# Accumulation ahead of the mixer steps, alternating PSUM banks, and a long convolution over 13 weight items: one change to a two-block kernel on one core

## The reference, cut to what matters

```
# block 1: h = x + token_mixer(rms_norm(x)); h = h + conv_gated_mlp(rms_norm(h)); rms_norm
proj = n @ w_in                       # per head: q,k,v,z of a gated delta rule (4 tiles of 128),
                                      # and q,k,v of 3 dilated attentions (9 tiles)
mixed = concat(delta_mixer(...), dilated_mixer(...)) @ w_out
# block 2, modulated: shift, scale and gate from two condition vectors
m = silu(c) @ w_ada + b_ada           # 2048 x 12288, for two vectors c
u = modulate(rmsnorm(x), sh1, sc1);  p = u @ w_in_2
a = hgrn2_mixer(p[:5 parts], context) # per head 5 tiles
y = x0 * long_conv(x1 * v)            # "hyena", per head 3 tiles, by Fourier transforms
x = x + g1 * (concat(a, y) @ w_out_2);  x = x + g2 * mlp(modulate(rmsnorm(x)))
```

## Time and profile before

| | before |
|---|---|
| time, median of 3 runs | 3736.71 us (3734.02 to 3743.41) |
| profiled execution | 3737.85 us, of it span 3736.1 us |
| PE busy | 3350.2 us (90%) |
| DVE busy | 2304.9 us (62%) |
| ACT busy | 1557.9 us (42%) |
| POOL busy | 1427.2 us (38%) |
| DMA | 672.83 MB, mean 180 GB/s |

### The profile page before, as it was taken

How to read it: one execution, slowest core, us unless ns; L and a number is a source line. 1 busy time by engine, 2 the same in 40 slices (tenths; PEclk the granted TensorE clock), 3 DMA queues, 4 the chain that set the end, 5 groups by cost and what they waited for, 6 DMA issues and landing times.

```text
span 3736.1 us, 58829 instructions
## 1 busy us (share of the span) xinstructions
PE 3350.2 (90%) x21604; PEld 3013.0 (81%) x21604; DVE 2304.9 (62%) x3370; ACT 1557.9 (42%) x2196; POOL 1427.2 (38%) x672
## 2 busy tenths in 40 slices
PE   5898989898979999999987887888887999999998
PEld 4888988898877878878864886788887788888886
DVE  5676666766655883883874755666665654535353
ACT  4344333433334443443433554344433443434343
POOL 2334433343323444444431333344433344444442
PEclk7999999999999999999998998898988999999999
DMA  4655565556455555556544755565554655565553
GB/s 167 198 171 177 175 205 168 177 173 205 165 194 194 184 174 188 178 171 191 179 137 150 233 182 186 173 199 157 167 166 187 227 181 183 180 191 186 186 186 112
DMA packets 262366, 672.83 MB, mean 180 GB/s; under 512 B 28263, under 2 KB 66888, under 8 KB 261448
## 3 DMA queue, kind: packets, MB, share of 16 engines
q1 hardware_dynamic: 262152, 669.81, 54.7%
HBM read 663.38 MB, written 6.32 MB: 179 GB/s over the span
## 4 chain that ended last, share of the span: by engine, by line
PE 55%; DVE 18%; issue 14%; POOL 5%; ACT 4%; DMA 3%; SPq 1%; DVEq 1%; ACTq 0%; POOLq 0%
PE psum L633 20%; PE psum L634 10%; POOL w_lo L495 5%; PE psum L626 4%; PE psum L628 4%; PE psum L627 4%; ACT w_hi L485 2%; PE psum L703 2%; DVE w_lo L495 2%; DVE psum L476 1%; PE psum L631 1%; PE psum L1396 1%; PE psum L1405 1%; DVE work L1252 1%; DVE work L1631 1%
## 5 line engine op out<-in xcount | busy, mean ns | idle before, releaser
L495 POOL TENSOR_TENSOR w_lo<-raw,w_hi 128x1024 fp32r<-128x1024 f32 (+3 forms) x668 | 1427.0, 2139 | 2278.9 <-ACT w_hi L485 2278.1
L485 ACT ACTIVATE w_hi<-raw 128x1024 fp32r<-128x1024 f32 (+3 forms) x1112 | 1046.4, 947 | 1394.2 <-PE psum L628 663.8
L626 PE MATMUL psum<-act_a,w_lo 128*128 128x256 f32 x3072 | 929.1, 302 | 62.5 <-ACT work L663 36.8
L495 DVE TENSOR_TENSOR w_lo<-raw,w_hi 128x1024 fp32r<-128x1024 f32 (+3 forms) x444 | 541.4, 1219 | 576.9 <-ACT w_hi L485 575.0
L627 PE MATMUL psum<-act_a,w_hi 128*128 128x256 f32 x3072 | 891.7, 290 | 0.0
L628 PE MATMUL psum<-act_a,w_hi 128*128 128x256 f32 x3072 | 891.3, 290 | 0.0
L633 PE MATMUL psum<-act_a,w_hi 128*128 128x512 f32 x2295 | 829.6, 403 | 25.2 <-DVE act_a L745 10.6
L633 PE MATMUL psum<-act_b,w_hi 128*128 128x512 f32 x2096 | 754.6, 402 | 27.7 <-DVE act_b L1639 17.9
L626 PEld LDWEIGHTS psum<-act_a,w_lo 128*128 128x128 f32 x3072 | 612.6, 199 | 74.3 <-ACT work L663 32.9
L634 PE MATMUL psum<-act_a,w_lo 128*128 128x256 f32 x2295 | 648.1, 282 | 0.0
L627 PEld LDWEIGHTS psum<-act_a,w_hi 128*128 128x128 f32 x3072 | 612.8, 199 | 3.1 <-issue 1.9
(11 more groups left out here) (335 smaller groups left out, 3319.8 us busy)
## 6 DMA issues: line engine op xcount, KB each, us to landing
raw<-w_mlp SPq DMA_DIRECT2D x256, 512.0 KB, 3.8
raw<-w_up SPq DMA_DIRECT2D x176, 512.0 KB, 3.5
raw<-w_dil SPq DMA_DIRECT2D x192, 384.0 KB, 3.4
work<-w_ada SPq DMA_DIRECT2D x288, 256.0 KB, 4.0
raw<-w_hg SPq DMA_DIRECT2D x128, 320.0 KB, 3.0
raw<-w_delta SPq DMA_DIRECT2D x64, 512.0 KB, 3.9
raw<-w_out SPq DMA_DIRECT2D x64, 512.0 KB, 5.9
raw<-w_down SPq DMA_DIRECT2D x64, 512.0 KB, 3.6
```

The costliest lines, as they stand in the source:

```text
L485: act.activation(w_hi[:, t % SPLIT, 0:nb * P], raw[:, t % RAW, 0:nb * P], ACT.Copy)\
L495: eng.tensor_tensor(w_lo[:, t % SPLIT, 0:nb * P], raw[:, t % RAW, 0:nb * P], w_hi[:, t % SPLIT, 0:nb * P], ALU.subtract)\
L626: pe.matmul(bank[:, 0:S], wl, src[:, kt, 0:S], start=first, stop=False)
```

## The change

1. `Phase("one", ..., unroll=2)`, and `bank` with two banks adds the head's parity: head 0 puts tiles 0, 1, ... 12 into banks 0, 1, ... 0, head 1 into banks 1, 0, ... 1. `bank_free_after` asks for the last tile of the head before in the same bank. With 8 tiles a head, `two` keeps its banks.
2. On DVE the accumulation steps of an item stand at its start, ahead of the split and the mixers. In `one` the places move from items 2 to 15 (two in 6 and 11) to 3 to 15 (two in 5, 9 and 13), in the pair phases (`ctx`, `out`, `out2`) similarly; in `two` they stay at 0 to 15. `ADA_LAG` is 7 for 8.
3. `ada_finish` takes 3 steps instead of 2: ACT in the first, PE and DVE in the third. In `two` it starts at item 18 instead of 16.
4. The convolution takes 13 items instead of 6: DVE's steps in items 1, 5, 7, 10 and 12 (were 0, 2, 3, 4, 5), PE's in 4, 6 and 9 (were 2, 3, 4), ACT's in 11 (was 4). Its spectra are loaded at SP's item 20 (was 16).

```diff
-ADA_SLOTS, ADA_LAG = 4, 8
+ADA_SLOTS, ADA_LAG = 4, 7
...
-            at = [p for p in range(2, 16) for _ in range(2 if p in (6, 11) else 1)]
+            at = [p for p in range(3, 16) for _ in range(2 if p in (5, 9, 13) else 1)]
...
-            at = range(8) if par else (2, 3, 4, 4, 5, 6, 6, 7)
+            at = range(8) if par else (3, 4, 4, 5, 5, 6, 6, 7)
...
-        last = max(q for q in range(self.tpb) if self.bank(q) == self.bank(k))
+        last = max(q for q in range(self.tpb) if self.bank(q, 1 - self.par) == self.bank(k))
...
-    def bank(self, k):
+    def bank(self, k, par=None):
+        if self.banks == 2:
+            return (k + self.tpb * (self.par if par is None else par)) % 2
...
-        Phase("one", NH, [("w_delta", 8)] * 8 + [("w_dil", 6)] * 24, [KT] * 13, banks=2),
+        Phase("one", NH, [("w_delta", 8)] * 8 + [("w_dil", 6)] * 24, [KT] * 13, banks=2, unroll=2),
...
                 for t in range(ph.ipb):
+                    for idx, (at, _, _) in enumerate(ph.ada_plan(ph.par) if ada else ()):
+                        if at == t:
+                            ada_step(eng, ph, i, idx)
                     if t + AHEAD < ph.ipb:
                         split(eng, ph, i, t + AHEAD)
...
                     for q in range(2):
                         hop(live, q)
-                    for idx, (at, _, _) in enumerate(ph.ada_plan(ph.par) if ada else ()):
-                        if at == t:
-                            ada_step(eng, ph, i, idx)
...
-            return [(0, 6, 1, hyena(eng), -1), (16, 2, 1, ada_finish(who, eng, ph), 0),
+            return [(0, 13, 1, hyena(eng), -1), (18, 3, 1, ada_finish(who, eng, ph), 0),
                     (13, 11, 1, lambda i: hgrn(ph.late)(i), 0)]
...
-            return [(0, 2, 1, ada_finish(who, eng, ph, 1), -1), (0, 8, 1, dilated(eng), -1),
-                    (16, 2, 1, ada_finish(who, eng, ph, 0), 0), (3, 29, 1, delta(eng), 0)]
+            return [(0, 3, 1, ada_finish(who, eng, ph, 1), -1), (0, 8, 1, dilated(eng), -1),
+                    (16, 3, 1, ada_finish(who, eng, ph, 0), 0), (3, 29, 1, delta(eng), 0)]
```

More of the change, by code:

```diff
@@ L573, in body @@
                         if not (first and off < 0):
+                            par, ph.par = ph.par, (ph.par + off) % 2
                             evac(i + off, k)
+                            ph.par = par
                     live = [m for m in live if m[0] > t] + mixers.start(t, i, first)
@@ L588, in drive @@
                 if off < 0:
+                    ph.par = (ph.n - 1) % 2
                     evac(ph.n - 1, k)
+                    ph.par = 0
             mixers.finish(ph.n)
@@ L837, in act @@
                 yield
+                yield
             def pe(i):
+                yield
                 yield
@@ L2176, in gen @@
             def gen(i):
-                for _ in range(4):
+                for _ in range(11):
                     yield
@@ L2187, in gen @@
             def gen(i):
-                yield
-                yield
+                for _ in range(4):
+                    yield
                 pe.wait_ge(sem("two_loaded"), 16 * TWO_LOADS)
@@ L2280, in one_mixers @@
             ph = PHD["one"]
-            return [(0, 2, 1, ada_finish(who, eng, ph, 1), -1), (0, 8, 1, dilated(eng), -1),
-                    (16, 2, 1, ada_finish(who, eng, ph, 0), 0), (3, 29, 1, delta(eng), 0)]
+            return [(0, 3, 1, ada_finish(who, eng, ph, 1), -1), (0, 8, 1, dilated(eng), -1),
+                    (16, 3, 1, ada_finish(who, eng, ph, 0), 0), (3, 29, 1, delta(eng), 0)]
         def pair_mixers(who, eng, ph):
-            return [(0, 2, 1, ada_finish(who, eng, ph), -1)]
+            return [(0, 3, 1, ada_finish(who, eng, ph), -1)]
         block = es.enter_context(nc.Block())
```

2 lines of the change are left out of this document (1 added, 1 removed).

## The result

The changed kernel takes 3694.67 us (median of 4 runs, 3688.78 to 3700.39), the kernel before 3738.21 us on the same chip: ratio 0.9887, 95% interval 0.9869 to 0.9906. That is 42 us less, 1.1%, where 85 were forecast. The profiled execution has a span of 3696.1 us, 40.0 less than before.

The account below looks back on a forecast made before the run. PE, busy 3350.2 of 3736.1 us, was taken to bound the kernel, so gains come from its idle or half-clock time. 3737.85 - 47 - 10 - 28 = 3653, put at 3652 us for the median; range 3610 to 3710.

Parts of the forecast that it names:

- Part A: Phase `one`, head boundaries: alternating banks remove PE's copy-out wait, leaving a 1.9 us scores wait at full clock; 47 us.
- Saved: 6.7 us ... 7 boundaries: 7 x 6.7: Phase `one`: item 1 ends at about 313.1 instead of 319.78 us, at each of 7 boundaries; 47 us.
- moves from item 1 to item 2, ahead of the 5.95 us wait on L1310, which covers it: Phase `one`: L845, the row's turning on PE, 0.95 us at full clock, was to be hidden in that wait.
- Part B: Phase `two`, row of modulation: later finish removes the 5.4 us wait at the row's turning; 1.3 us a head, 10 us.
- So a wait of 5.1 us replaces one of 5.4 ... 1.3 us a head: Phase `two`: PE waits for DVE's products at L2072 instead of the row; 8 heads, 10 us.
- My bounds (-3 to +45): Row of modulation in `two`: -3 us without DVE's earlier chain, +45 with early products and the clock staying up.
- Part C: Phase `two`, convolution over 13 items: transposes' wait falls to 3.6 us, clock likely up; 4.0 us in 7 heads, 28 us.
- What was to cost nothing: Accumulations ahead of splits, weight loads, w_ada loads one item earlier, pair phases, moved copy L2180: 0 us.
- Rival (5): DVE waits for a w_ada transfer ahead of a split PE needs; slower, 3801 us at 8.5 us each; chance 0.05.
- Rival (3): Waits only change names: banks gain 27 us, row loses 3, convolution gains 7; 3707 us; chance 0.20.
- 3610 to 3710: Whole kernel's time: range holding the as-worked-out case, most of the waits-change-names case and nearer part of the waits-vanish case.

Follow-up runs that it names:

- e5_acc_behind: Changed kernel with DVE's accumulations put behind the mixer steps again, all else as changed: ratio 0.9836.
- e1_banks: Kernel before with the alternating banks in `one` alone: 3704.76 us against 3740.85, ratio 0.9901.
- e9_two_early: Changed kernel with the old finish (two steps, from item 16) in phase `two` only: 3664.24 us, ratio 0.9805.
- e3_acc: Changed kernel with banks and convolution of before; accumulations ahead, lag 7, new places, three-step finish and item 18 kept: 3759.60 us, ratio 1.0053.
- e2_conv: Kernel before with the convolution over 13 items and its spectra at item 20 alone: 3698.99 us, ratio 0.9886.
- e10: Changed kernel with the old finish in `two` and the accumulations behind the mixer steps: 3654.17 us against 3739.35 before, ratio 0.9768.
- e6: Kernel before with the alternating banks and the 13-item convolution together, nothing else: 3666.51 us, ratio 0.9791.
- e7: Changed kernel with the two-step finish of before in all phases, from item 16 in `two`: ratio 0.9823.
- e12: Changed kernel with `two`'s splits of items 20 and 21 moved from POOL to DVE, item 23's from DVE to POOL: 3665.11 us, ratio 0.9808.
- e8: Changed kernel, POOL computing `w_lo` of five items a head in `two` for one block only, output partly wrong: one execution, 3653 us.

## Why the prediction was wrong in size and right in sign

**Part A (47 us, came to 33.2; the banks alone 38.9).** The mechanism held: no copy-out waits, scores waiting 2.0 us in five heads, clock at 1.00 behind them. What failed are two steps, "Saved: 6.7 us ... 7 boundaries: 7 x 6.7" and L845, which "moves from item 1 to item 2, ahead of the 5.95 us wait on L1310, which covers it".

The 6.7 us were read off one head. From L1386 (lines of before) to the end of item 1 (ACT's split behind L1532) that head took 81.2 us, but the seven took 80.3 on average. In the changed kernel it is 74.6, near the 74.5 that the forecast implies, so 5.7 us are saved and not 6.7: 7 us in seven heads. In these 74.6 lies a new wait of 0.8 us a head at L1432, since an accumulation now stands ahead of the copy that PE needs; e5_acc_behind, without it, takes 73.4 to 73.9 us in five heads. In the other two it takes 75.7, with the clock at 0.72 behind the scores.

L845 is covered only in part. From the end of item 1 to the next L1386 it is 44.6 us before and in e1_banks, which doesn't move it, and 45.1 in most heads of e5_acc_behind and of the changed kernel, which do. The wait at L1396 stays at 5.9 us. That is 0.5 us in six heads: 3 us.

In two heads, behind the loop's back edge, that second stretch takes 47.6 us. PE waits 2.10 us instead of 1.34 at L1597 and goes on at half clock (its twelve products take 4.54 us for 2.87): 2 x 2.4 = 5. So 47 - 7 - 3 - 5 = 32, and 33.2 were measured. Timelines of DVE and PE at L1432, changed kernel:

```profile
403.00 0.73 DVE L478 SCALAR_TENSOR_TENSOR psum<-work,ada_c,psum 128x512 f32<-128x512 f32 x1
403.65 0.41 DVE L1337 COPY work<-psum 128x256 f32<-128x256 f32 x1
...
404.11 0.71 PE L1432 MATMUL psum<-work 128*128 128x128 f32 x4 [0.80 <-DVE work L1337]
```

e1_banks and e5_acc_behind have no such wait and take 837 us in `one`.

**Part B (10 us, came to a loss: 9 us against before, and some 27 beside part C).** This is the step that failed most: "So a wait of 5.1 us replaces one of 5.4 ... 1.3 us a head". Two things were wrong in it. I put the end of L2002 15.6 us behind the start of L2061 (2382.4 less 2366.8); measured are 17.7 us (2354.97 less 2337.30). The first product starts 0.5 us later than I had it, and a second one meets POOL's splits (1.6 us), where I had carried over one. I knew the collisions and priced them in part C, but took DVE's chain here as merely moved. And the half clock that the row's wait leaves had a use: it lay ahead of the products while DVE computed them, and in the changed kernel the half clock follows them, with nothing to cover.

The step behind the products (L2087 of before) was to come 2.3 us earlier behind L2061 (3.8 less 1.5). It comes at 23.5 us in the mean of eight heads, against 23.3 before, and L853's 0.95 us in item 20 comes on top: a loss of 9 us where 10 were to be won. Beside part C the price is higher, since there e9_two_early, with the old finish, has this step at 21.0 us: 8 x (2.5 + 0.95) = 28 us, against 25.3 read between the two for the whole phase. e3_acc, without part C, lost 17 us in the heads, the order's cost included. My bounds (-3 to +45) left the value out.

**Part C (28 us; 41 alone).** The waits came as forecast: 3.39 to 3.67 us in seven heads, 8.02 in the last, none at the inverse transform but there. The clock did not stay up behind 3.39 us (0.68 in the window). The surplus lies in a stretch that part C didn't count. From L2061 to L2087 (lines of before) e2_conv takes 20.9 us in the mean of eight heads, against 23.3 before, which is 19 of the 41 us; the other 22, on the transposes' side, are fewer than the 28 forecast. Of the 19, 9 are the row's shorter wait. In the 6 us behind that wait the clock was at 0.72 in six of eight heads (one is 2381.58 to 2387.58 us), and before at 0.50 to 0.54 in all. In the head that I compared DVE's copies and scans also met POOL less often (L1969 0.16 us for 1.66, L1982 0.69 for 2.13). In the changed kernel this gain is gone, by part B.

**What was to cost nothing.** That the accumulations "lie in its waits for PE" is wrong: their order costs 14 to 19 us (e9 to e10, changed kernel to e5). One piece is plain. At the start of `two` DVE stands 10.4 us at the first accumulation, whose loaded piece isn't there yet, ahead of a split for PE (timelines of DVE and PE):

```profile
2240.55 0.75 DVE L475 TENSOR_SCALAR psum<-raw,ada_c 128x512 f32<-128x512 f32 x1 [10.38 <-issue]
2241.22 2.03 DVE L497 TENSOR_TENSOR w_lo<-raw,w_hi 128x640 fp32r<-128x640 f32 x1
...
2243.30 0.58 PE L632 MATMUL psum<-act_a,w_lo 128*128 128x256 f32 x1 [13.61 <-DVE w_lo L497]
```

Before, DVE waited as long at that accumulation, but behind the split. The list of waits had the line:

```profile
DVE psum L473 <- DMA raw<-w_ada: 10.5, 1, 10.5
```

Rival (5) had this mechanism, but read only L476's waits, 2.8 us at most, and so said that the longest was far below 7.2 us. One such wait occurred, not 48; it passed the 7.2 us and cost 4 to 5 us, net of PE's usual waits at that place. Rival (3), that waits only change their names, was right about B and worse than priced there, and wrong about A and C.

**The sum.** By stretches of the changed kernel against before: 33 for A (with the order's cost in `one`), 22 on the transposes' side for C, -9 for B's stretch, -4.5 for the first items, together 42; the profiled spans differ by 40.0. All three parts came out below their terms, and one that was put at nothing cost time. That 3694.67 us still lay inside 3610 to 3710 says nothing for the terms: B's was outside its own bounds, and the range was kept wide for waits that only change their names.

**What stays open.** Phase `one` took 836.9 us in e1 and 843.4 in e6, whose code is the same there. At least one source is seen in e6 (timelines of DVE, POOL and PE):

```profile
443.37 2.74 DVE L497 TENSOR_TENSOR w_lo<-raw,w_hi 128x1024 fp32r<-128x1024 f32 x1
...
443.22 1.81 POOL L497 TENSOR_TENSOR w_lo<-raw,w_hi 128x768 fp32r<-128x768 f32 x1 [2.27 <-ACT w_hi L487]
...
447.42 4.55 PE L1593 MATMUL psum<-work 128*128 128x256 f32 x12 [3.72 <-DVE work L1522]
```

In e1 the same split takes 1.22 us and PE waits 1.28 us. What decides whether the two engines meet there was not tried. e7's phase `one` is 13 us longer than e9's. Its trace shows where: PE waits 16.9 us at L1593 in seven heads, mostly 2.05 us each, against 1.35 in most heads of e9, and the clock behind is at 0.50 to 0.66 in five heads, while e9 has the slow clock there in two. Why its finish in two steps makes that wait longer was not tried.

## What to carry to other kernels

Before moving a step that PE waits for, look at what its wait and the slow clock behind it cover; the next step's producer may need just that time. An operation put ahead of another engine's input can cost its whole length there, however idle its engine is on average (0.8 us at each L1432), and at a phase's start its DMA's wait. Read a saving off all heads and not off one, and look at the longest wait of every line of a step, not only of the commonest. Measure parts of a change apart: here two were worth 78 us together and the third took 36 of them away.

## What the runs showed of the hardware

DVE and POOL meet as if one held the other up to its end: in e6 POOL's split ends at 445.03 us, and DVE's, started at 443.37, at 446.11, which is POOL's end and 1.08 us, against 1.22 us alone. *SBUF — State Buffer*, section "SBUF: two separate sides", in the Trainium skill, says that the shared port pair is an exclusive lock for a whole instruction; this row agrees, and so do e12's products of 0.69 us with POOL idle and e8's of 0.69 and 0.95 us with POOL's splits short. New to me was how far it decides the time: with five short splits a head, e8's phase `two` was 39.5 us shorter.

The length of a wait alone didn't tell what PE's clock did. Behind 2.02 us at L1571 it was at 1.00 (2.4 GHz); behind 2.10 us at L1597 in the head behind the back edge it was at 0.62 (445.66 to 450.20 us), with full clock and an unbroken stream in the 10.8 us ahead of the wait; behind 1.34 us at the same line it was at 1.00. In e5_acc_behind 2.03 us at L1571 was followed by 0.72 in one head (299.51 to 305.51 us) and by 1.00 in another (538.84 to 544.84 us), and the first cost it 2 us. The same wait of 3.69 us for the row was followed by 0.72 in one head of e10 (2608.05 to 2614.10 us) and 0.50 in the next (2674.53 to 2680.00 us).
